# Experts with at most 96 tokens as three rounds of 32 tokens, each in four column tiles of TensorE

## The chip, the cores and the metric

The kernel runs on one core of a Trainium2 chip. The metric is the device time of one execution in microseconds (us), from the first to the last instruction and what lies around it; lower is better.

## The reference, cut to what matters

One decoder layer on 1024 tokens of width 1024, all in float32: a mixer (projections, short convolution, sliding-window attention, output projection) and then a mixture of 32 experts, of which each token takes four. The experts are what the change touches:

```python
logits = h @ w_router + b_router                  # (1024, 32)
top_vals, top_idx = lax.top_k(logits, 4)
gates = softmax(top_vals)
# for every expert e, on the tokens routed to it:
hid = xb @ w1[e] + b1[e]                          # (n, 1024) @ (1024, 2048)
x_glu, x_lin = hid[..., ::2], hid[..., 1::2]
x_glu = min(x_glu, 7); x_lin = clip(x_lin, -7, 7)
act = x_glu * sigmoid(1.702 * x_glu) * (x_lin + 1)
yb = (act @ w2[e] + b2[e]) * gate                 # (n, 1024) @ (1024, 1024)
out[token] += yb
```

Evaluated on its own inputs, the reference routes 4096 token-expert pairs. The 32 experts get, sorted: 66, 80, 81, 93, 95, 95, 100, 101, 106, 113, 114, 122, 122, 123, 125, 126, 128, 134, 136, 136, 136, 137, 138, 140, 148, 152, 161, 163, 165, 172, 187, 201 tokens. So 15 have more than 128, 11 have 97 to 128, and 6 have at most 96.

## The kernel before, in words

`mixer` runs first, in eight blocks of 128 tokens. Two of its places serve later as comparisons. `route_quarters` (line 889) makes the router's logits with 32 stationary columns in each of four column tiles of TensorE, every tile with its own moving data of 128 columns. `attend` (L921) does the same with 64 stationary columns in two column tiles and 512 moving columns.

`experts` then runs one job for each expert (at most 256 tokens a job). Jobs are sorted on the chip by a key (L1463 to L1487), large ones first: `size` counts the limits 128, 136, ..., 208 that an expert's tokens exceed, the key is `past - 128 * size`, and `reached` compares the keys with `marks`, so that every engine reads from `ends` and `jobs` how many jobs there are of each kind. Jobs with over 128 tokens are wide: weights stationary, tokens moving (`piece`, L1686). Jobs with at most 128 are narrow, and run last: tokens stationary, 128 columns, weights moving. The work of one narrow job:

- SP (SyncE) loads w1 in four pieces of 2 MB (each 512 of the 2048 columns, all 1024 rows, in runs of 2 KB) and w2 in two such pieces into the six slots of `w_slot` (`load_pieces`, L1235). The load for a slot is issued when TensorE has used it (`w_used`), so weights arrive one job ahead. b1 and b2 are spread over 128 partitions (L1256, L1259).
- TensorE, `first_layer` (L1710): for each of the four chunks c, eight matmuls (k = 0..7) of 128x128 stationary x, 512 moving columns. Every float32 matmul stands in the trace as two MATMUL records, called passes below. `list_rows` (L1699) makes the token list of the next job between chunks 1 and 2. `second_layer` (L1722): eight matmuls of 512 columns for each half of the output. The last two k of both halves wait for the last chunk, turned by TensorE (`turn_last`, L1732).
- VectorE, for each chunk: add b1 (L1589), clip (L1593, L1594), multiply with ScalarE's sigmoid (L1601, L1604), and, but for the last, turn the rows into `act_T` by 32x32 transposes (L1216). After chunk 1 it takes over the next list (L1626 to L1582), which lets POOL (GpSimd) gather the next job's rows (L1293). At the end it turns the gathered rows into `xT` (L1216, `turn_x`), adds the gated b2 (L1636), and marks the tokens of the job after next (L1567 to L1572).
- ScalarE: sigmoids (L1394), the copy of the last chunk (L1397), b2 times gate (L1400).
- POOL adds the result to the output by an indirect DMA (L1337).

```python
def narrow_job(t, q):                 # TensorE, L1735
    first_layer(t, q, 0)
    first_layer(t, q, 1)
    list_rows(q + 1)
    first_layer(t, q, 2)
    first_layer(t, q, 3)
    second_layer(t, q, 0, range(0, KD - 2))
    turn_last(t)
    second_layer(t, q, 1, range(0, KD - 2))
```

## Time and profile before

| what | value |
|---|---|
| median of 3 runs | 2027.83 us (2026.98 to 2029.89) |
| the profiled execution, its own time | 2026.62 us |
| its span, first to last instruction | 2024.8 us |
| mean granted TensorE clock | 0.989 of 2.4 GHz |
| TensorE busy | 1970.9 us (97%) |
| from the first narrow job's start to the 17th's (1297.25 to 1966.87 us) | 669.6 us |

In a windows row stand the length, the busy us of PE, PEld, DVE, ACT and POOL with their counts, the granted clock, the DMA share and GB/s. A row of "busy" for TensorE counts modelled, overlapping ends: one pass of 512 columns is drawn as 592 ns, but the next one starts 429 ns after it. So durations below are taken between starts. In a timeline row the first number is the start, the second the length of the merged stretch, and "x32" the number of records in it; PE is the matmul side of TensorE and PEld its weight loads. DMA share is the mean busy share of the 16 DMA engines; overlapping packets can take it over 1.

### The profile page before, as it was taken

How to read it: one execution, taken by the hardware profiler on the slowest of the kernel's cores; microseconds unless marked ns; L12 is line 12 of the kernel's file. 1: busy time of each engine (PE TensorE's matmuls, PEld its weight loads, DVE VectorE, ACT ScalarE, POOL GpSimd, SP SyncE). 2: the span in 40 equal slices, each digit the busy share in tenths (PEclk: the TensorE clock that was granted, in tenths of full speed). 3: DMA queues.
4: the chain of work that ended last, by engine and by line, in shares of the span. 5: the costliest groups of instructions: out<-in, count | busy, mean ns of one | idle time of the engine just before them, and what ended most of it. 6: DMA issues, size and time to landing. Idle time of an engine off the chain costs nothing.

```text
span 2024.8 us, 29838 instructions
## 1 busy us (share of the span) xinstructions
PE 1970.9 (97%) x10536; PEld 1434.4 (71%) x10536; DVE 1424.0 (70%) x4050; ACT 402.7 (20%) x848; POOL 237.0 (12%) x317
## 2 busy tenths in 40 slices
PE   7999999997999999999999999999999999999996
PEld 5677777774999999999999999744444444444442
DVE  2777777764467777778766776777667776777765
ACT  1233333232012112222222223211100010000100
POOL 1221222221010011111111111100000000000000
PEclk8999999998999999999999999999999999999998
DMA  9311110004866778787788888999999999999992
GB/s 308 105 42 41 41 33 20 31 32 177 305 219 210 263 249 269 246 273 266 258 293 281 299 290 306 327 329 370 361 354 372 367 368 362 356 368 370 370 355 74
DMA packets 232238, 504.17 MB, mean 249 GB/s; under 512 B 7428, under 2 KB 14640, under 8 KB 230016
## 3 DMA queue, kind: packets, MB, share of 16 engines
q1 hardware_dynamic: 218496, 454.93, 62.9%
q0 software_dynamic: 11392, 40.18, 8.1%
q10 hardware_dynamic: 2304, 8.39, 1.0%
q8 instruction: 35, 0.57, 0.1%
q14 instruction: 11, 0.09, 0.0%
HBM read 475.48 MB, written 28.00 MB: 249 GB/s over the span
## 4 chain that ended last, share of the span: by engine, by line
issue 41%; PE 11%; DMA 1%; POOL 1%; DVE 1%; POOLq 0%; ACT 0%
PE ps_unit L1686 11%; DMA out_dram<-y_rows,idx_cur 1%; POOL x_got L1293 1%; DVE act_T L1515 0%; DVE sig L1513 0%; DVE glu L1505 0%; ACT sig L1376 0%; POOL carrier L1289 0%; POOL out_dram L1337 0%; POOL out_dram L1305 0%; PE ps_list L1658 0%; POOLq L1065 0%; POOLq L1227 0%; POOLq L1328 0%; DMA x_got<-h_rows,idx_next 0%
## 5 line engine op out<-in xcount | busy, mean ns | idle before, releaser
L1686 PE MATMUL ps_unit<-xT,w_slot 128*128 128x136 f32 (+6 forms) x3840 | 523.1, 299 | 1.6 <-DVE xT L1540 1.6
L1686 PEld LDWEIGHTS ps_unit<-xT,w_slot 128*128 128x128 f32 x3840 | 518.2, 197 | 2.0 <-issue 1.8
L1710 PE MATMUL ps_unit<-w_slot,xT 128*128 128x512 f32 x1088 | 473.9, 593 | 0.0
L1710 PEld LDWEIGHTS ps_unit<-w_slot,xT 128*128 128x128 f32 x1088 | 205.3, 190 | 251.6 <-issue 251.6
L1216 DVE STREAM_TRANSPOSE xT<-x_got 32x256 f32<-32x256 f32 x668 | 291.0, 436 | 15.9 <-DMA x_got<-h_rows,idx_next 7.1
L1686 PE MATMUL ps_unit<-act_T,w_slot 128*128 128x136 f32 (+6 forms) x1920 | 264.1, 299 | 10.4 <-DVE act_T L1515 10.3
L1686 PEld LDWEIGHTS ps_unit<-act_T,w_slot 128*128 128x128 f32 x1920 | 259.3, 191 | 13.9 <-DVE act_T L1515 7.3
L1722 PE MATMUL ps_unit<-w_slot,act_T 128*128 128x512 f32 x544 | 239.3, 592 | 1.3 <-DVE act_T L1216 1.3
L1216 DVE STREAM_TRANSPOSE act_T<-act_rows 32x64 f32<-32x64 f32 x816 | 192.6, 236 | 12.2
L1531 DVE STREAM_TRANSPOSE y_rows<-yT 32x256 f32<-32x256 f32 x396 | 172.6, 436 | 39.6 <-ACT yT L1383 34.4
L1722 PEld LDWEIGHTS ps_unit<-w_slot,act_T 128*128 128x128 f32 x544 | 102.0, 190 | 123.6 <-issue 121.5
L899 PE MATMUL ps_c<-hT,w_in_sb 128*128 128x128 f32 x1536 | 182.1, 279 | 4.5 <-DMA w_in_sb<-in_w_in_dram 4.5
L899 PEld LDWEIGHTS ps_c<-hT,w_in_sb 128*128 128x128 f32 x1536 | 177.4, 194 | 9.7 <-DMA w_in_sb<-in_w_in_dram 5.3
L1289 POOL TENSOR_TENSOR carrier<-carrier 128x1 f32<-128x1 f32 x64 | 14.9, 233 | 1362.0 <-issue 572.7
L1394 ACT ACTIVATE sig<-glu 128x256 f32<-128x256 f32 x68 | 28.3, 416 | 553.6 <-DVE glu L1593 553.6
L1589 DVE TENSOR_TENSOR hid<-ps_unit,b_row 128x512 f32<-128x512 f32 x68 | 47.0, 691 | 84.5 <-PE ps_unit L1710 84.4
L1513 DVE TENSOR_TENSOR sig<-sig,glu 128x256 f32<-128x256 f32 x120 | 50.9, 424 | 69.6 <-ACT sig L1376 61.3
L1376 ACT ACTIVATE sig<-glu 128x256 f32<-128x256 f32 x120 | 50.0, 417 | 243.6 <-DVE glu L1505 243.4
L1505 DVE TENSOR_SCALAR glu<-ps_unit,b_cur 128x256 f32<-128x256 f32 x120 | 57.5, 479 | 52.5 <-PE ps_unit L1686 52.0
L1383 ACT ACTIVATE yT<-ps_unit,b_cur 128x256 f32<-128x256 f32 x120 | 50.3, 469 | 210.2 <-PE ps_unit L1686 210.2
L1388 ACT ACTIVATE y_rows<-y_rows,gate_cur 128x1024 f32<-128x1024 f32 x30 | 32.8, 1141 | 179.5 <-DVE y_rows L1531 179.5
L1636 DVE SCALAR_TENSOR_TENSOR y_rows<-ps_unit,gate_cur,b_row 128x512 f32<-128x512 f32 x34 | 25.5, 751 | 59.8 <-PE ps_unit L1722 59.8
(267 smaller groups left out, 1648.4 us busy)
## 6 DMA issues: line engine op xcount, KB each, us to landing
w_slot<-in_w_dram SPq DMA_DIRECT2D x192, 2048.0 KB, 10.9
b_row<-in_b_dram SPq DMA_DIRECT2D x17, 1024.0 KB, 12.8
b_row<-in_b_dram SPq DMA_DIRECT2D x17, 512.0 KB, 15.1
w_in_sb<-in_w_in_dram SPq DMA_DIRECT2D x6, 1024.0 KB, 12.0
x_in<-in_x_dram SPq DMA_DIRECT2D x8, 512.0 KB, 3.5
x_res<-in_x_dram SPq DMA_DIRECT2D x8, 512.0 KB, 4.8
out_dram<-x ACTq DMA_DIRECT2D x8, 512.0 KB, 5.1
h_rows<-h ACTq DMA_DIRECT2D x8, 512.0 KB, 3.2
```

The lines of the kernel that those rows point to most:

```text
L899: last = pe.matmul(ps_c[:, c % 2, j * P:(j + 1) * P], w_in_sb[:, k, first:first + P], hT[:, k, :], start=(k == 0), stop=(k == KD - 1))
L1216: last = nc.vector.transpose(out[c * Q:(c + 1) * Q, :, tokens], rows.rearrange("p (k c j) -> p k c j", c=P // Q, j=Q)[:, :, c, :])
L1376: nc.scalar.activation(sig[:, p % 3, :], glu[:, p % 3, :], ACT.Sigmoid, scale=ALPHA).then_inc(sig_ready[p].sem, 1)
L1383: last = nc.scalar.activation(yT[:, m, :], ps_unit[p % RING][:, u, :], ACT.Identity, bias=b2_cur[:, m:m + 1])
L1388: last = nc.scalar.activation(y_rows[:, h, :], y_rows[:, h, :], ACT.Copy, scale=gate_cur[:, h:h + 1])
L1505: v.tensor_scalar(glu[:, p % 3, :], ps_unit[p % RING][:, 0, :], b1_cur[:, 2 * p:2 * p + 1], LIMIT, ALU.add, ALU.min).then_inc(glu_ready[p] ...
L1513: v.tensor_tensor(sig[:, p % 3, :], sig[:, p % 3, :], glu[:, p % 3, :], ALU.mult).then_inc(scaled[p].sem, 1)
L1531: last = v.transpose(rows[:, :, c, :], yT[c * Q:(c + 1) * Q, :, a * Q:(a + 1) * Q])
L1589: v.tensor_tensor(hid[:, c % 2, :], ps_hid[c], b1_row[:, c * LW:(c + 1) * LW], ALU.add).then_inc(hid_read[c].sem, 1)
L1686: last = pe.matmul(ps_unit[p % RING][:, u, 0:n], w, moving[:, k, 0:n], start=(k == 0), stop=(k == KD - 1))
L1710: last = pe.matmul(ps_hid[c], xT[:, k, 0:P], w_slot[:, c, k, :], start=(k == 0), stop=(k == KD - 1))
L1722: last = pe.matmul(ps_out[m], act_T[:, k, 0:P], w_slot[:, W1_LOADS + m, k, :], start=(k == 0), stop=(k == KD - 1))
```

## The change

Jobs with at most 96 tokens ("slim") get a kind of their own, between wide and narrow. A slim job's 96 token columns are three rounds t of 32 tokens. In a round, the 32 columns of x stand in four column tiles of the array at once (`tile_position=(0, g * 32)`), and tile g gets as moving data the g-th quarter of the weight's columns: 512 of w1, 256 of w2. The result of a round stands in one PSUM bank, partitions 32g to 32g+31 for tile g. The first layer's k loop is outermost up to k = 5, so that weights come as whole rows (runs of 8 KB for w1, 4 KB for w2). b1 is spread as four quarters over 32 partitions each, b2 over 96. The rows of a round are turned by TensorE and copied by ScalarE, VectorE's `act_T` transposes are gone; ScalarE moves the second layer's result, quarter by quarter, into `y_rows`. The sorting gets one more mark, and every engine one more job count.

```diff
+TILE = 32
+TILES = 3
+SLIM = TILES * TILE
...
+                        src = w1[0, bass.ds(e, 1), 2 * i * P:2 * (i + 1) * P, :].rearrange("o (k p) f -> p (o k) f", p=P)
+                        sp.dma_start(w_slot[:, i, :, :].rearrange("p (k c) f -> p k (c f)", k=2), src).then_inc(w_loaded[i].sem, 16)
...
+                    nc.gpsimd.indirect_dma_start(
+                        out=out_rows, out_offset=bass.IndirectOffsetOnAxis(ap=idx_cur[0:SLIM, 0:1], axis=0),
+                        in_=y_rows[0:SLIM, 0, :], in_offset=None, compute_op=ALU.add).then_inc(rows_moved.sem, 16)
...
+            def slim_read_act(s, t):
+                wait_round(act, slim_turned, s, t)
+                nc.scalar.copy(act_T[:].rearrange("p (g r) n -> p r g n", r=2)[:, :, :, t * TILE:(t + 1) * TILE],
+                               ps_act[:, 0:2, :].rearrange("p r (g n) -> p r g n", g=W1_LOADS)).then_inc(slim_actT.sem, 1)
...
+                for g in range(W1_LOADS):
+                    last = nc.scalar.copy(y_rows[t * TILE:(t + 1) * TILE, 0, g * PW:(g + 1) * PW],
+                                          ps_flat[TILES + t][g * TILE:(g + 1) * TILE, 0:PW])
...
+                    slim_sigmoid(s, 0)
+                    slim_sigmoid(s, 1)
+                    slim_read_act(s, 0)
+                    slim_sigmoid(s, 2)
+                    slim_read_act(s, 1)
...
+            then_wait(v.scalar_tensor_tensor(out=slim[:], in0=first[:], scalar=float(SLIM), in1=held[:], op0=ALU.add,
+                                             op1=ALU.is_ge))
+            then_wait(v.scalar_tensor_tensor(out=past[:], in0=slim[:], scalar=-float(P // 2), in1=past[:], op0=ALU.mult,
+                                             op1=ALU.add))
...
+                    wait(dve, gate_summed, q)
+                    wait(dve, pool_moved, wide - 1)
+                    wait(dve, rows_moved, s - 1)
+                    v.tensor_copy(idx_cur[:, 0:1], idx_next[:, 0:1])
...
+                    read_narrow_list(q + 1)
+                    for t in range(TILES):
+                        slim_clip_round(s, q, t)
+                        slim_finish_round(s, t)
+                    wait(dve, gathered_a, q + 1)
+                    turn_x(q + 1, P // Q)
+                    match_narrow(q + 2, bass.ds(e_next, 1), base_row[:, bass.ds(q + 2, 1)])
+                    wait(dve, slim_b2, s)
+                    wait_round(dve, slim_out_read, s, TILES - 1)
+                    v.scalar_tensor_tensor(out=y_rows[0:SLIM, 0, :], in0=y_rows[0:SLIM, 0, :], scalar=gate_cur[0:SLIM, 0:1],
...
+            def slim_first(t, k):
+                i, f = k // 2, k % 2
+                for g in range(W1_LOADS):
+                    w = w_slot[:, i, :, :].rearrange("p (k c) f -> p k (c f)", k=2)[:, f, g * LW:(g + 1) * LW]
+                    last = pe.matmul(ps_flat[t][g * TILE:(g + 1) * TILE, :], xT[:, k, t * TILE:(t + 1) * TILE], w,
+                                     start=(k == 0), stop=(k == KD - 1), tile_position=(0, g * TILE))
...
+                for k in range(KD - 2):
+                    if k % 2 == 0:
+                        wait(pe, w_loaded[k // 2], q)
+                    for t in range(TILES):
...
+                        last = slim_first(t, k)
...
+                    if k == 3:
+                        list_rows(q + 1)
+                wait(pe, w_loaded[W1_LOADS - 1], q)
+                for t in range(TILES):
+                    for k in (KD - 2, KD - 1):
+                        last = slim_first(t, k)
+                    last.then_inc(round_done.sem if t < TILES - 1 else w_used[W1_LOADS - 1].sem, 1)
+                slim_turn(s, 0)
+                slim_second(s, q, 0, range(0, 4))
+                slim_turn(s, 1)
+                slim_second(s, q, 0, range(4, KD))
+                slim_second(s, q, 1, range(0, 4))
+                slim_turn(s, 2)
+                slim_second(s, q, 1, range(4, KD))
+                slim_second(s, q, 2, range(0, KD))
```

`slim_turn` transposes a round's `act_rows` in two transposes of 128x128 into `ps_act`; `slim_second` is the second layer of a round, four matmuls of 256 columns for each k, one in each column tile; `slim_clip_round` and `slim_finish_round` are `clip_rows` and `finish_rows` for a round.

## Rows read from the trace of the kernel before

**Rows 1.** Page, part 1 and part 2: engines' shares; the span in 40 slices.
```profile
PE 1970.9 (97%) x10536; PEld 1434.4 (71%) x10536; DVE 1424.0 (70%) x4050; ACT 402.7 (20%) x848; POOL 237.0 (12%) x317
...
PEclk8999999998999999999999999999999999999998
DMA  9311110004866778787788888999999999999992
```
**Rows 2.** Windows: first narrow job, fifteen narrow jobs, 10 us (us, busy by engine, clock, DMA).
```profile
1297.25:1341.22 43.97, 42.19 (x108) 18.45 (x107) 36.33 (x110) 8.67 (x12) 4.34 (x5) 1.00 0.87 302
1341.22:1966.87 625.65, 625.65 (x1591) 279.16 (x1590) 451.19 (x1515) 65.53 (x105) 45.28 (x60) 1.00 1.02 365
1620.00:1630.00 10.00, 10.00 (x26) 4.54 (x25) 8.36 (x21) 3.12 (x4) 0.00 (x0) 1.00 1.06 392
```
**Rows 3.** Timeline of PE, one narrow job (columns: start, length, as above).
```profile
1508.06 13.90 PE L1710 MATMUL ps_unit<-w_slot,xT 128*128 128x512 f32 x32
1521.79 0.35 PE L1699 MATMUL ps_list<-entry,match 128*128 128x5 bf16 x8
1522.00 13.98 PE L1710 MATMUL ps_unit<-w_slot,xT 128*128 128x512 f32 x32
...
1540.97 0.38 PE L1732 MATMUL ps_act<-cst,act_rows 128*128 128x128 f32 x2
1541.18 8.75 PE L1722 MATMUL ps_unit<-w_slot,act_T 128*128 128x512 f32 x20
```
**Rows 4.** Timeline of PE in the mixer: two and four column tiles, and neighbours.
```profile
416.52 1.95 PE L899 MATMUL ps_c<-hT,w_in_sb 128*128 128x128 f32 x16
418.39 0.65 PE L889 MATMUL ps_s<-h2T,w_router_sb 128*32 128x128 f32 x16
418.97 0.71 PE L899 MATMUL ps_c<-hT,w_in_sb 128*128 128x128 f32 x4
...
444.09 1.94 PE L921 MATMUL ps_c<-pT,v_keys 128*64 128x512 f32 x8 [0.45 <-DVE pT L716]
445.95 1.55 PE L993 MATMUL ps_s<-w_out_sb,conv_s 128*128 128x512 f32 x3
```
**Rows 5.** Timeline of DVE and ACT in that narrow job.
```profile
1521.99 0.69 DVE L1589 TENSOR_TENSOR hid<-ps_unit,b_row 128x512 f32<-128x512 f32 x1 [0.33 <-PE ps_unit L1710]
...
1529.15 0.69 DVE L1589 TENSOR_TENSOR hid<-ps_unit,b_row 128x512 f32<-128x512 f32 x1
1529.88 0.29 DVE L1593 TENSOR_SCALAR glu<-hid 128x256 f32<-128x256 f32 x1
...
1531.64 3.98 DVE L1216 STREAM_TRANSPOSE act_T<-act_rows 32x64 f32<-32x64 f32 x16
...
1537.07 0.42 ACT L1394 ACTIVATE sig<-glu 128x256 f32<-128x256 f32 x1 [6.45 <-DVE glu L1593]
...
1538.39 7.17 DVE L1216 STREAM_TRANSPOSE xT<-x_got 32x256 f32<-32x256 f32 x16
...
1548.34 0.75 DVE L1636 SCALAR_TENSOR_TENSOR y_rows<-ps_unit,gate_cur,b_row 128x512 f32<-128x512 f32 x1 [2.77 <-PE ps_unit L1722]
...
1541.38 0.37 ACT L1397 COPY act_T<-ps_act 128x256 f32<-128x256 f32 x1 [3.90 <-PE ps_act L1732]
```
**Rows 6.** Timeline of POOL: the last scatter of the last wide job.
```profile
1312.30 1.33 POOL L1305 DMA_INDIRECT out_dram<-y_rows,idx_cur  x1 [0.30 <-issue]
```
**Rows 7.** DMA view from 1341 to 1967 us: KB each, median us to landing.
```profile
w_slot<-in_w_dram SPq DMA_DIRECT2D x90, 2048.0 KB, 13.1
out_dram<-y_rows,idx_cur POOLq DMA_INDIRECT x15, 9.9
x_got<-h_rows,idx_next POOLq DMA_INDIRECT x15, 7.0
```
**Rows 8.** Timeline of DVE in the sorting of the jobs.
```profile
476.47 0.16 DVE L1467 TENSOR_TENSOR past<-past,cst 128x1 f32<-128x1 f32 x1
476.66 0.16 DVE L1468 SCALAR_TENSOR_TENSOR order_key<-size,past 128x1 f32<-128x1 f32 x1
```

More of the change, by code:

```diff
@@ L1116, in experts @@
         order = sb("order", [P, P], BF16)
-        ends = sb("ends", [1, len(SIZES) + WORDS], I32)
-        ended, started, first, held, size, past = (sb(n, [P, 1]) for n in ("ended", "started", "first", "held", "size", "past"))
+        ends = sb("ends", [1, COLUMNS + WORDS], I32)
+        ended, started, first, held, size, past, slim = (
+            sb(n, [P, 1]) for n in ("ended", "started", "first", "held", "size", "past", "slim"))
         ps_unit = [ps(f"ps_unit{i}", [P, 2, CAP]) for i in range(RING)]
@@ L1207, in job_counts, with wait_round @@
             wide = eng.value_load(ends[0:1, last_size - 1:last_size], min_val=0, max_val=most_jobs)
+            slim_jobs = eng.value_load(jobs[0:1, 2:3], min_val=0, max_val=most_jobs)
             narrow_jobs = eng.value_load(jobs[0:1, 1:2], min_val=0, max_val=most_jobs)
-            return wide, narrow_jobs
+            full = eng.value_load(ends[0:1, len(SIZES):COLUMNS], min_val=0, max_val=most_jobs)
+            return wide, slim_jobs, narrow_jobs, full
+        def wait_round(eng, e, jobs_done, t):
+            eng.wait_ge(e.sem, e.of(jobs_done * e.per, t))
         def turn_squares(out, rows, tokens):
@@ L1238, in _ @@
             sp.wait_ge(rows_moved.sem, 16)
-            wide, narrow_jobs = job_counts(sp)
+            wide, slim_jobs, narrow_jobs, full = job_counts(sp)
             with sp.If(wide > 0):
@@ L1315, in _ @@
             get(gathered_b, 1, P)
-            wide, narrow_jobs = job_counts(pool)
+            wide, slim_jobs, narrow_jobs, full = job_counts(pool)
             with pool.If(wide > 0):
@@ L1648, in _ @@
             with dve.If(narrow_jobs > 0):
                 with dve.Fori(0, narrow_jobs) as t:
[L1650 removed]
+                    narrow_job(t, t + full)
         @block.tensor
@@ new lines, in slim_second @@
+            def slim_second(s, q, t, ks):
+                if ks[0] == 0:
+                    wait(pe, unit_read[RING + TILES + t], wide - 1)
+                    wait_round(pe, slim_out_read, s - 1, t)
+                    wait_round(pe, slim_actT, s, t)
+                for k in ks:
+                    i, f = W1_LOADS + k // 4, k % 4
+                    if t == 0 and f == 0:
+                        wait(pe, w_loaded[i], q)
+                    for g in range(W1_LOADS):
+                        w = w_slot[:, i, :, :].rearrange("p (k c) f -> p k (c f)", k=4)[:, f, g * PW:(g + 1) * PW]
+                        last = pe.matmul(ps_flat[TILES + t][g * TILE:(g + 1) * TILE, 0:PW], act_T[:, k, t * TILE:(t + 1) * TILE], w,
+                                         start=(k == 0), stop=(k == KD - 1), tile_position=(0, g * TILE))
+                    if t == TILES - 1 and f == 3:
+                        last.then_inc(w_used[i].sem, 1)
+                if t < TILES - 1 and ks[-1] == KD - 1:
+                    last.then_inc(slim_out.sem, 1)
@@ L1834, in _ @@
+            with pe.If(slim_jobs > 0):
                 with pe.If(wide < 1):
                     first_rows()
+                with pe.Fori(0, slim_jobs) as s:
+                    slim_job(s, s + wide)
+            full = wide + slim_jobs
+            with pe.If(narrow_jobs > 0):
+                with pe.If(full < 1):
+                    first_rows()
                 with pe.Fori(0, narrow_jobs) as t:
-                    narrow_job(t, t + wide)
+                    narrow_job(t, t + full)
```

203 lines of the change are left out of this document (171 added, 32 removed).

## The prediction

> **What bounds the kernel now.** First the page's parts 1 and 2: TensorE is busy in 97% of the span, at full clock over the part that matters (the last third of the slices), and the DMA engines stand at nine tenths or more there too [rows 1]. So one asks which of the two ends last. The windows of the narrow stage answer: in fifteen whole narrow jobs, 625.65 us, TensorE has no idle time, 625.65 / 15 = 41.71 us a job, while the DMA moves 365 GB/s at a share of 1.02, and in its best 10 us 392 GB/s [rows 2]. The timeline shows that TensorE's time is the passes alone: 32 passes of 512 columns from 1508.06 to 1521.79, that is 0.429 us each, 96 of them in a job (41.2 us), 0.21 us for the list and 0.21 us for the turn [rows 3]. A pass costs its moving columns, whether 66 or 128 of the 128 stationary columns hold tokens. TensorE is the bound, the DMA queue is close behind. VectorE's 451 us in those 625.65 are covered [rows 2].
>
> The reference's own routing gives 6 experts with at most 96 tokens, 11 with 97 to 128. So 6 of the 17 narrow jobs become slim; they come first, the first of them right behind the last wide job. The other 26 jobs keep their code.
>
> **TensorE's share of a slim job.** Removed: 96 passes. Added: in the first layer 3 rounds times 8 k, each k-step four matmuls of 512 columns, one in each column tile. If four tiles really run at once, a k-step costs two passes, 0.859 us: 24 x 0.859 = 20.6 us instead of 27.5. The second layer has 24 k-steps of 256 columns, 0.429 us each: 10.3 us instead of 13.7. In sum 30.9 us instead of 41.2.
>
> Do they run at once? Two rows show tiles with separate moving data. With four tiles and 128 columns, 16 passes take 418.97 - 418.39 = 0.58 us, where the 16 full-array passes of the same width ahead of them take 416.52 to 418.39, 0.117 us each; four at a time would be 0.47, so 0.11 us is over. With two tiles and 512 columns, 8 passes take 1.86 us, and two at a time would be 1.72: 0.14 over [rows 4]. The excess is nearly the same for a block of 0.5 and of 1.8 us, so I read it as a price of entering and leaving tiled work, 0.14 us a block, and the sharing itself as full. That is the value I take; from below nothing under 0.859 us is possible for 512 columns in one tile, from above no sharing would be four times that.
>
> The Trainium skill speaks against this: "TensorE: Matmul & The Clock Gate", section "Part 3: Packing small matmuls — row/col tiling", has three column tiles of 512 columns at 2.38 times and four row tiles at 3.07 times one, that is 0.77 to 0.79 of full. By it a k-step would cost 1.3 times what I take and a slim job would be no shorter than a narrow one; the traced blocks show no such loss, but both are short. It is the first rival below.
>
> Full-array work inside the tiled work: the list (0.21 us) and three turns of two transposes (0.21 us each), each with 0.14 us for the change-over, 0.35 us a block [rows 3, 4]. With the list the first layer ends at 20.6 + 0.35 = 20.95 us after the job's start. Then one wait is open. Round 0 is complete four k-steps earlier, at 17.5; VectorE picks a finished bank up 0.20 us after the next passes begin, and needs 1531.64 - 1529.15 = 2.49 us a round [rows 3, 5]: rounds end at 20.2, 22.7 and 25.2. TensorE turns round 0 by 21.3, but ScalarE's copy into `act_T` is queued behind the sigmoid of round 1, for which VectorE must first add and clip (0.69 + 0.29 from 20.2): sigmoid 0.42 to 21.7, copy 0.37 to 22.1 [rows 5]. So the second layer begins 1.2 us after the first, the turn of round 0 included. The turns of rounds 1 and 2 come when their rows have long been ready (24.2 against 22.7, 28 against 25.2) and cost 0.35 us each. Sum: 20.95 + 1.2 + 10.3 + 0.7 = 33.2 us.
>
> **What must stay covered.** VectorE loses the three `act_T` transposes (3.98 us each) [rows 5]. Its chain to the next `xT` is 25.2 + 7.17 = 32.4 us, against TensorE's 33.2: covered by 0.8 us. That needs the next rows to be there by 25.2. The chain for them: behind the last pass ScalarE copies four quarters (4 x 0.37), VectorE adds b2 over 1024 columns (about 2 x 0.75 us) [rows 5], POOL issues the addition, which lands 9.9 us later [rows 7], about 13.6 us into the next job. Only then may VectorE overwrite `idx_cur`, which now stands ahead of its first round, take the list, and let POOL gather: 7.0 us [rows 7], landed at about 21.3, 3.9 us in time. `idx_cur` itself is free at 13.6, round 0 wants VectorE at 17.7. ScalarE's twelve copies of 0.37 us and its sigmoids are under 10 us a job. All this is covered, but by few us where now it is tens.
>
> **The DMA.** A narrow job moves 6 x 2048 KB of weights, 1536 KB of biases, 1024 KB of rows: 15.2 MB, which is 365 GB/s over 41.71 us, so the view is accounted for [rows 2, 7]. A slim job moves 12288 + 256 + 384 + 512 + 384 KB = 14.2 MB: 38.8 us at 365 GB/s, 36.1 us at 392. Both exceed 33.2, so the queue falls behind by 3 to 6 us with each slim job. It has a cushion: loads are issued a job ahead, the last slots are freed at the end of a job and wanted 22 us into the next, which with the job's own length leaves some 24 us, against 13.1 us to landing now [rows 7]: 11 us to spare, more for the first slots. Over the five loads behind slim jobs 12 to 25 us may gather, so a stall of 0 to 14 us at their end is possible. Longer runs (8 and 4 KB for 2 KB) may shift the rate either way; no row shows by how much. I take 0.6 us a job, 3 us in all, for this and late gathers: 33.8 us a slim job. SP's extra issues (four for b1) stand behind the load of slot 3 and ahead of slots that are freed 10 us later; the wait for the b2 row (3.2 us into a job) comes ahead of slot 0's release at 5.2.
>
> **The first slim job** meets the scatter of the last wide job: it must have landed (1312.30 + 9.9 = 1322.2, 24.9 us into the job [rows 6, 7]) ahead of VectorE's round 0, where before it stood after chunk 1. Round 0 then ends at 28.0, the copy at 29.9, the job at 29.9 + 10.3 + 0.7 = 40.9 us; before, that first job took 43.97 [rows 2]. Saved: 3.1. The sorting adds two dependent VectorE steps at a cadence of 0.19 us [rows 8], two more small ones and one register load per engine: between 0 (hidden behind the gather of the first rows) and 2 us; I take 1.0.
>
> **Sum.** 5 x (41.71 - 33.8) + 3.1 - 1.0 = 41.6 us. The profiled execution took 2026.6 us, 1.2 us under the median: 1985.0 on its basis, 1986.2 on that of the median, and 1986 is what I forecast.
>
> **Rivals.**
> 1. *The tiles share worse in long runs.* Place: the 48 k-steps. A job is then 30.9 f + 2.3 us, and it decides at f = (41.7 - 2.3) / 30.9 = 1.27. At f = 1.3 a job is 42.5 us and the first, whose VectorE wait is then covered, also 42.5: 5 x 0.8 - 1.5 + 1.0 = 3.5 us slower, 2031 us; with tiles two at a time (f = 2) 64.1 us a job, 2160 us. For it: no row has four tiles with 512 columns, each moving stream being read at once. Against: the four-tile block and the two-tile block show an excess that doesn't grow with length [rows 4]. 0.09.
> 2. *The supply ends last*: the DMA keeps 365 GB/s and its cushion is gone at once, or the scatter-gather chain with 3.9 us to spare is late. A slim job is then 38.8 us: 5 x 2.9 + 3.1 - 1.0 = 16.6 us saved, 2011 us; half of it 1998. For it: a share of 1.02 already now [rows 2]. Against: the cushion, and fewer bytes. 0.14.
> 3. *Short instructions bind.* The second layer wants a weight load and a pass every 54 ns. The row of the list has 8 such pairs in 0.21 us, 26 ns each, straight behind long passes [rows 3]: nothing against it, but they came from a filled queue. The Trainium skill, "TensorE: Matmul & The Clock Gate", section "Wait — 56ns, not 53.3ns?", gives 62 ns a matmul where the sequencer decodes in software; by it the second layer would be 11.9 us and the forecast 8 us higher, 1994 us. At half of the list's pace, 52 ns, it costs nothing. It lies inside the forecast's own range and has no separate time there; 0.05 of its chance.
> 4. *The change doesn't take hold*: the sort on the chip counts none as slim. 2029 us, 0.03. The counts nearest to 96 are 95 and 100, far for rounding.
>
> **The numbers.** Forecast 0.74, rival 2 0.14, rival 1 0.09, rival 4 0.03. The forecast's own range is 1974 (no allowance, waits half of what I charge, the first job without its wait) to 1998; to hold 8 in 10 the range takes in rival 2: 1974 to 2011. About 0.2% (4 us) is what a measurement can tell from no change. Faster 0.74 + 0.14 = 0.88, same 0.03, slower 0.09.
>
> **What the profile after would show.** Right: six stretches of about 33 to 35 us, 192 passes of 512 columns and 192 of 256 in each, the start of a k-step 0.86 and 0.43 us after the last one's; about 1.2 us of TensorE's idle time behind the first layer; the first slim job near 41 us. Wrong: k-steps above 1.09 us (rival 1); TensorE waiting for `w_slot` or `xT` (rival 2); k-steps of the second layer alone above 0.43 us (rival 3); 17 jobs with 128 stationary columns (rival 4).

## The result and the profile after

The changed kernel takes 2001.68 us (median of 4 runs, 1999.35 to 2003.95), the kernel before 2028.06 us beside it (4 runs): ratio 0.9871, 95% interval 0.9859 to 0.9883. It is faster by 26 us, 1.3%, where 42 were forecast. In the two profiled executions the spans are 1997.6 and 2024.8 us, 27.2 us apart.

First the page of the kernel after, parts 1 and 2. It looks like that of before [rows 1]: TensorE at 96%, the DMA at nine tenths in the last third. What is new stands in slices 28 to 32: 379 to 399 GB/s, where before there were 354 to 372.

```profile
span 1997.6 us, 33413 instructions
...
PE 1923.2 (96%) x12288; PEld 1402.9 (70%) x12288; DVE 1342.6 (67%) x3731; ACT 430.5 (22%) x926; POOL 236.0 (12%) x317
...
PEclk9999999999999999999999999999999999999998
DMA  9311101013867777777788888889999999999992
GB/s 309 109 42 42 42 12 41 31 32 119 327 204 243 255 244 268 255 264 259 265 278 287 287 305 290 311 300 381 399 388 379 382 364 358 365 368 368 366 356 74
```

The last line of the kernel before:

```profile
GB/s 308 105 42 41 41 33 20 31 32 177 305 219 210 263 249 269 246 273 266 258 293 281 299 290 306 327 329 370 361 354 372 367 368 362 356 368 370 370 355 74
```

The windows of the six slim jobs and the two narrow jobs behind them (cut where TensorE begins a job's first layer; the columns are us, then busy us and instructions by engine, granted clock, DMA share, GB/s) answer to [rows 2]:

```profile
1298.62:1341.10 42.48, 35.03 (x399) 13.67 (x402) 22.77 (x60) 10.42 (x20) 4.34 (x5) 0.92 0.80 292
1341.10:1374.67 33.57, 32.97 (x402) 13.13 (x398) 17.33 (x54) 8.95 (x20) 2.88 (x4) 1.00 1.00 381
...
1441.84:1475.41 33.57, 32.97 (x402) 13.12 (x398) 16.38 (x48) 9.06 (x20) 2.85 (x4) 1.00 1.02 394
1475.41:1510.92 35.51, 33.16 (x402) 13.00 (x394) 16.62 (x49) 9.06 (x20) 2.86 (x4) 1.00 1.03 381
1510.92:1564.32 53.40, 47.11 (x110) 20.28 (x107) 28.91 (x91) 7.10 (x12) 2.85 (x4) 0.90 1.04 385
1564.32:1606.03 41.71, 41.71 (x107) 18.61 (x106) 30.08 (x101) 4.37 (x7) 3.02 (x4) 1.00 1.03 374
```

So the first slim job takes 42.48 us, the next four 33.58 each, the sixth 35.51. And the first *narrow* job behind them takes 53.40 us, though its code is that of the others, which take 41.71 as before. The account in spans: the small jobs start 1.4 us later than before (1298.62 against 1297.25); the first six of them take 212.3 us instead of 252.5, so 40.2 saved; the seventh costs 11.7 more. 40.2 - 11.7 - 1.4 = 27.1 us.

Where the idle time in this is, TensorE's waits say (from 1298 us on: what it executed, on what it waited, us in all, times, longest):

```profile
PE ps_act L2052 <- DVE act_rows L1802: 6.5, 1, 6.5
PE ps_unit L1907 <- DVE act_T L1262: 6.3, 2, 3.8
PE ps_unit L2040 <- issue: 4.0, 6, 1.0
PE ps_unit L2040 <- DMA w_slot<-in_w_dram: 1.8, 1, 1.8
```

TensorE's timeline of the first slim job's end, the second one up to its second layer, and the first narrow job (start, us, and in brackets the idle time ahead and what ended it) stands beside [rows 3]:

```profile
1326.32 0.69 PE L2052 MATMUL ps_act<-cst,act_rows 128*128 128x128 f32 x2 [6.46 <-DVE act_rows L1802]
1328.00 3.64 PE L2040 MATMUL ps_unit<-w_slot,act_T 128*32 128x256 f32 x32 [0.99 <-issue]
...
1341.10 10.48 PE L2024 MATMUL ps_unit<-w_slot,xT 128*32 128x512 f32 x96
1351.52 0.35 PE L1877 MATMUL ps_list<-entry,match 128*128 128x5 bf16 x8
1351.80 10.51 PE L2024 MATMUL ps_unit<-w_slot,xT 128*32 128x512 f32 x96
1362.24 0.44 PE L2052 MATMUL ps_act<-cst,act_rows 128*128 128x128 f32 x2
1363.28 1.93 PE L2040 MATMUL ps_unit<-w_slot,act_T 128*32 128x256 f32 x32 [0.60 <-issue]
...
1510.92 14.00 PE L1894 MATMUL ps_unit<-w_slot,xT 128*128 128x512 f32 x32
...
1538.78 1.88 PE L1907 MATMUL ps_unit<-w_slot,act_T 128*128 128x512 f32 x4
1543.17 3.68 PE L1907 MATMUL ps_unit<-w_slot,act_T 128*128 128x512 f32 x4 [2.51 <-DVE act_T L1262]
1550.63 3.78 PE L1907 MATMUL ps_unit<-w_slot,act_T 128*128 128x512 f32 x4 [3.78 <-DVE act_T L1262]
1554.20 0.63 PE L1917 MATMUL ps_act<-cst,act_rows 128*128 128x128 f32 x2
1554.63 9.86 PE L1907 MATMUL ps_unit<-w_slot,act_T 128*128 128x512 f32 x20
```

Two things are to be seen. The slim job's four tiles share fully: a k-step of the first layer is eight of these passes (two for each of its four matmuls), and 96 passes in 10.44 us make 0.870 us a k-step, where two full-array passes take 0.859. And idle time is paid twice: behind it the same four passes take 3.68 us instead of 1.88, at the lower level of the clock. The granted clock of these stretches is 0.50 behind the first slim job's gap and 0.52 behind the narrow job's:

```profile
1328.00:1331.50 3.50, 3.50 (x32) 1.54 (x32) 2.54 (x7) 0.42 (x1) 0.00 (x0) 0.50 1.00 410
1543.17:1546.70 3.53, 3.53 (x4) 1.17 (x4) 2.64 (x11) 0.42 (x1) 1.19 (x2) 0.52 1.05 387
```

In the first narrow job TensorE idles 6.29 us and is busy for 47.11 instead of 41.71: 6.3 + 5.4 = 11.7 us.

TensorE names VectorE as the one it waited for; VectorE's own timeline passes it on, to the 1 MB of the narrow job's b1 row, issued at 1510.5 and landed at 1530.1, 16 us after VectorE was free for it and 12.3 us after TensorE had the first chunk ready (1517.8):

```profile
1530.14 0.69 DVE L1716 TENSOR_TENSOR hid<-ps_unit,b_row 128x512 f32<-128x512 f32 x1 [16.28 <-DMA b_row<-in_b_dram]
```

### The profile page after: what moved, and what is told of

Read it like the earlier page. It is cut to its first block, busy times and chain, and to the rows that moved or that the text cites. A ratio compares the mean times of both kernels' runs of the same rounds, so it can differ in the third digit from the quotient of the medians.

```text
span 1997.6 us, 33413 instructions
## 1 busy us (share of the span) xinstructions
PE 1923.2 (96%) x12288; PEld 1402.9 (70%) x12288; DVE 1342.6 (67%) x3731; ACT 430.5 (22%) x926; POOL 236.0 (12%) x317
## 4 chain that ended last, share of the span: by engine, by line
issue 38%; PE 13%; POOL 1%; DMA 1%; DVE 1%; POOLq 0%; ACT 0%
PE ps_unit L1864 13%; DMA out_dram<-y_rows,idx_cur 1%; POOL x_got L1361 1%; DVE act_T L1642 0%; DVE sig L1640 0%; DVE glu L1632 0%; ACT sig L1457 0%; POOL carrier L1357 0%; PE ps_list L1836 0%; POOL out_dram L1418 0%; POOL out_dram L1373 0%; POOLq L1081 0%; POOLq L1273 0%; DMA x_got<-h_rows,idx_next 0%; POOLq L1409 0%
## 5 line engine op out<-in xcount | busy, mean ns | idle before, releaser
L1894 PE MATMUL ps_unit<-w_slot,xT 128*128 128x512 f32 x704 | 306.7, 594 | 0.0
L1894 PEld LDWEIGHTS ps_unit<-w_slot,xT 128*128 128x128 f32 x704 | 132.8, 190 | 163.0 <-issue 163.0
L1907 PE MATMUL ps_unit<-w_slot,act_T 128*128 128x512 f32 x352 | 159.8, 607 | 6.3 <-DVE act_T L1262 6.3
L1262 DVE STREAM_TRANSPOSE act_T<-act_rows 32x64 f32<-32x64 f32 x528 | 124.6, 236 | 7.9
L1907 PEld LDWEIGHTS ps_unit<-w_slot,act_T 128*128 128x128 f32 x352 | 67.4, 195 | 88.3 <-issue 79.7
L2024 PE MATMUL ps_unit<-w_slot,xT 128*32 128x512 f32 x1152 | 126.0, 593 | 0.0
L1457 ACT ACTIVATE sig<-glu 128x256 f32<-128x256 f32 x120 | 50.0, 417 | 242.3 <-DVE glu L1632 242.1
L1475 ACT ACTIVATE sig<-glu 128x256 f32<-128x256 f32 x44 | 18.3, 416 | 371.9 <-DVE glu L1720 371.9
L2024 PEld LDWEIGHTS ps_unit<-w_slot,xT 128*32 128x32 f32 x1152 | 36.7, 110 | 80.1 <-issue 79.2
L1716 DVE TENSOR_TENSOR hid<-ps_unit,b_row 128x512 f32<-128x512 f32 x44 | 30.4, 692 | 68.0 <-PE ps_unit L1894 51.7
## 6 DMA issues: line engine op xcount, KB each, us to landing
w_slot<-in_w_dram SPq DMA_DIRECT2D x192, 2048.0 KB, 11.7
```

The costliest lines, as they stand in the source:

```text
L1262: last = nc.vector.transpose(out[c * Q:(c + 1) * Q, :, tokens], rows.rearrange("p (k c j) -> p k c j", c=P // Q, j=Q)[:, :, c, :])
L1457: nc.scalar.activation(sig[:, p % 3, :], glu[:, p % 3, :], ACT.Sigmoid, scale=ALPHA).then_inc(sig_ready[p].sem, 1)
L1716: v.tensor_tensor(hid[:, c % 2, :], ps_hid[c], b1_row[:, c * LW:(c + 1) * LW], ALU.add).then_inc(hid_read[c].sem, 1)
L1894: last = pe.matmul(ps_hid[c], xT[:, k, 0:P], w_slot[:, c, k, :], start=(k == 0), stop=(k == KD - 1))
L1907: last = pe.matmul(ps_out[m], act_T[:, k, 0:P], w_slot[:, W1_LOADS + m, k, :], start=(k == 0), stop=(k == KD - 1))
L2024: last = pe.matmul(ps_flat[t][g * TILE:(g + 1) * TILE, :], xT[:, k, t * TILE:(t + 1) * TILE], w, start=(k == 0), stop=(k == KD - 1), tile_ ...
```

## The experiments

Two theories stood at the start. **A, the queue:** slim jobs ask for bytes faster than the DMA brings them; the loads fall behind job by job, and what has least time between issue and use shows it first, at the end of the slim jobs. **B, the hand-over:** the change from slim to narrow costs by itself, whatever ran before. Ratios are to the kernel before on the same chip. Its own median was 2028.5 us beside the first four kernels, 2029.6 beside the next three, 2027.3 beside the last four, so medians of different groups can't be compared to better than some 2 us; the spans from the start of the small jobs to the end of the profiled executions are the finer measure. In the changed kernel that is 1997.6 - 1298.6 = 699.0 us.

**Three slim jobs instead of six.**

```diff
-            then_wait(v.scalar_tensor_tensor(out=slim[:], in0=first[:], scalar=float(SLIM), in1=held[:], op0=ALU.add,
+            then_wait(v.scalar_tensor_tensor(out=slim[:], in0=first[:], scalar=82.0, in1=held[:], op0=ALU.add,
```

> Only experts with at most 82 tokens are slim: three slim jobs and fourteen narrow ones instead of six and eleven; nothing else changes. Theory A (queue): every slim job leaves the loads some 2.7 us further behind, so after three of them the first narrow job finds its b1 row in time. First slim job 42.5 us, the next two 33.58 us, no wait for a weight slot, first narrow job 41.7 to 43 us instead of 53.4. Time: 2001.7 + 3 x (41.71 - 33.58) - 11.7 - 1.75 = about 2012.6 us, so three slim jobs fewer cost only 11 us. Theory B (hand-over): the change from slim to narrow costs some 11 us however many slim jobs ran before. First narrow job about 53 us again, time 2001.7 + 24.4 - 1.75 = about 2024 us.

Measured: 2012.15 us, ratio 0.9925 (0.9908 to 0.9941). The first narrow job takes 43.45 us, with one wait of 0.53 us and one of 0.51:

```profile
1434.84 3.60 PE L1907 MATMUL ps_unit<-w_slot,act_T 128*128 128x512 f32 x8
1438.97 1.98 PE L1907 MATMUL ps_unit<-w_slot,act_T 128*128 128x512 f32 x4 [0.53 <-DVE act_T L1262]
```

B falls: the same change of kind, and no 11 us. The run also prices the later slim jobs: the last three save (2012.15 - 2001.68) / 3 = 3.5 us each instead of 8.1.

**The first narrow job's b1 row ahead of its weights.** The slim jobs get a b1 buffer of their own.

```diff
...
+                e = expert_of(sp, full)
+                spread_b1(e)
+                narrow_loads(0, full, e, True)
...
-                last = v.tensor_tensor(hid[:, t % 2, :], ps_flat[t], b1_row[:, 0:LW], ALU.add)
+                last = v.tensor_tensor(hid[:, t % 2, :], ps_flat[t], b1_slim[:], ALU.add)
```

> Six slim jobs as in the changed kernel. The slim jobs' b1 rows get a buffer of their own, so that the b1 row of the first narrow job waits for no slim job and is issued ahead of that job's weight loads instead of behind three of them. Theory A: the row lands before VectorE wants it, the first narrow job takes 42 to 44 us instead of 53.4; 1 MB more stands ahead of the weights in the queue, so their loads may be late by 0 to 3 us. Time 1990 to 1993 us. Theory B (the change of kind costs by itself): first narrow job 53 us whatever the row does, time about 2002 us. A third: the queue as a whole is behind, and the late row only shows it first; then the weights' loads end the first narrow job's waits instead, and it takes 46 to 50 us, time 1995 to 1999 us.

Measured: 1998.62 us, ratio 0.9858 (0.9842 to 0.9875), not to be told from the changed kernel's; from the start of the small jobs it is 695.0 us, 4 less. The first narrow job now takes 41.81 us, and the second 50.30: the wait has moved by one job, to the next b1 row in the old place. VectorE's timeline:

```profile
1571.84 0.69 DVE L1726 TENSOR_TENSOR hid<-ps_unit,b_row 128x512 f32<-128x512 f32 x1 [14.77 <-DMA b_row<-in_b_dram]
```

So neither A's 1990 nor B's 2002 us; the third case, that the whole queue is behind, is nearest, though it was again the row and not the weights that came late.

**VectorE takes the token list over behind round 0.**

```diff
-                    v.tensor_copy(idx_cur[:, 0:1], idx_next[:, 0:1])
...
-                    read_narrow_list(q + 1)
                     for t in range(TILES):
                         slim_clip_round(s, q, t)
                         slim_finish_round(s, t)
+                        if t == 0:
...
+                            v.tensor_copy(idx_cur[:, 0:1], idx_next[:, 0:1])
...
+                            read_narrow_list(q + 1)
```

> Only VectorE's order in a slim job changes: the copies of the next job's token list and gates, which wait for GpSimd's scatter of the job before, stand behind round 0's two additions instead of ahead of them. In the first slim job that wait let TensorE idle 6.46 us. If the wait for the last wide scatter is what that job pays for, its idle time falls to about 3 us (round 1 then waits for the same scatter) and it takes about 39 us instead of 42.5; the others stay at 33.58 us. Time: 1998.5 us if the rest of the chain follows, 2001 to 2002 us if the queue gives it back at the sixth job or the first narrow one (theory A: what TensorE gains earlier, the late loads take back at the end of the stage).

A miss: 2018.04 us, ratio 0.9957 (0.9941 to 0.9973), 16 us slower than the changed kernel. The ten executions spread from 2009.61 to 2025.45 us, and the profile is of the fastest, so it accounts for only 9.3 us (708.3 us from the start of the small jobs to the end); what the slower ones lose besides was not seen. VectorE of the second slim job, then TensorE at the start of the third:

```profile
1362.93 0.15 DVE L1816 COPY idx_cur<-idx_next 128x1 int32<-128x1 int32 x1
...
1372.61 7.18 DVE L1262 STREAM_TRANSPOSE xT<-x_got 32x256 f32<-32x256 f32 x16 [4.28 <-DMA x_got<-h_rows,idx_next]
```

```profile
1380.13 12.14 PE L2025 MATMUL ps_unit<-w_slot,xT 128*32 128x512 f32 x96 [3.08 <-DVE xT L1262]
```

The list that is read there is also what GpSimd gathers the next rows by. In the changed kernel VectorE reads it 13.3 us into a slim job (1354.42 in the job begun at 1341.10), here 20.5 us (1363.17 in that begun at 1342.68). That sends the gather off late in *every* slim job, and TensorE waits for `xT` at the start of each following job: 1.8 us in the second slim job and the first narrow one, 3.1 to 3.5 us in the four between. The slim jobs behind the first take 37.5 to 39.5 us. In the first one the idle time only fell to 5.5 us, and it took 43.2 us where 39 were expected. At that slower pace the first narrow job takes 41.81 us: no backlog. The steady slim job, which the expectation left at 33.58, was the step overlooked.

**Slim jobs last.** The order is wide, narrow, slim.

```diff
...
             then_wait(v.scalar_tensor_tensor(out=slim[:], in0=first[:], scalar=float(SLIM), in1=held[:], op0=ALU.add,
-                                             op1=ALU.is_ge))
+                                             op1=ALU.is_lt))
...
```

On every engine the block of the narrow jobs stands ahead of that of the slim ones, with the semaphore counts that go with it.

> The narrow jobs run right after the wide ones and the slim jobs last; the work of each kind is the same. Theory A: no narrow job follows a stretch of slim ones, so the 11.7 us of the late b1 row are gone; the first slim job follows a narrow one and takes about 34 us instead of 42.5; the first narrow job takes 44 instead of 41.7 us; a late weight load of 1 to 3 us in the fifth or sixth slim job stays. The kernel's tail may be 0 to 2 us longer. Time: 2001.7 - 11.7 - 8.9 + 2.3 + 1.5 = about 1985 us. Theory B: the change from narrow to slim costs as much as that from slim to narrow, time about 1995 to 1998 us.

Measured: 1999.54 us, ratio 0.9863 (0.9847 to 0.9879), where A's reckoning had about 1985. No loss at the change (the last narrow job 41.80 us, the first slim one 33.51), so B is out in this direction too; but A's size was wrong. The loads come late inside the slim jobs now, from the third on, 11.6 us of waits for a slot in all. The stretch from 1851 to 1966 us is three slim jobs long, cut at the same place of a job each time. Its window, and its DMA view (share and GB/s in 40 slices, then packets):

```profile
1851.47:1965.67 114.20, 102.92 (x1194) 40.65 (x1195) 49.11 (x142) 27.14 (x60) 8.57 (x12) 0.96 1.02 374
```

```profile
DMA  9999999999999999999999999999999999999999
GB/s 303 277 413 416 428 416 433 372 312 283 364 409 406 359 242 369 416 416 425 422 428 362 265 365 406 412 389 231 331 422 425 416 425 425 386 259 319 409 409 407
DMA packets 8183, 42.74 MB, mean 374 GB/s; under 512 B 629, under 2 KB 629, under 8 KB 5111
```

This is a number that was missing: 42.74 MB in 114.20 us are 14.25 MB and **38.07 us a slim job** when, in this kernel, the supply alone sets the pace. TensorE needs 33.58, so each job adds 4.5 us of backlog, not 2.7. In the changed kernel the queue was quicker at the same share. Its window over the second to the sixth slim job:

```profile
1341.10:1510.92 169.82, 165.06 (x1994) 65.52 (x1986) 83.09 (x243) 44.98 (x100) 14.30 (x20) 1.00 1.02 386
```

At 386 GB/s the 14.25 MB take 36.9 us, which makes 3.3 us of backlog a job. What makes the two rates differ was not tried, so a slim job adds somewhere from 3.3 to 4.5 us. With 4.5 the changed kernel's loss comes out: if about three jobs' worth is cushion, three more jobs' 13.5 us stand against the 1.9 and the 11.7 us that were lost. That the two agree so closely is partly luck. The rate is that of another kernel. The cushion is fitted to the runs (in this one the waits begin in the third slim job already), and 5.4 of the 11.7 us are TensorE's slower passes and not a wait for bytes. The runs with three and with six slim jobs put it a little lower: 1.9 us lost with three (the first narrow job 43.45 us, the third slim job 33.69), 13.6 with six, 3.9 us for each of the last three.

**Fewer bytes, the same work.** Left out: half of the second layer's weights in the slim jobs; the old contents of the slots stand in for them.

```diff
...
-                        src = w2[0, bass.ds(e, 1), 4 * i * P:4 * (i + 1) * P, :].rearrange("o (k p) f -> p (o k) f", p=P)
...
+                        src = w2[0, bass.ds(e, 1), 4 * i * P:(4 * i + 2) * P, :].rearrange("o (k p) f -> p (o k) f", p=P)
...
```

> Leaves out half of the second layer's weights in the slim jobs: each of their two second-layer loads brings two of its four k-blocks (1 MB instead of 2 MB), and the old contents stand in for the rest; TensorE, VectorE, ScalarE and GpSimd do exactly the same work. Supply theory, as the runs so far sharpen it: a slim job of 33.58 us asks for 14.2 MB, which take the saturated queue 38.07 us, so each slim job adds 4.5 us of backlog; three jobs' worth is cushion and the other three come out as 1.75 + 11.7 us of waits. With 12.2 MB a job the queue needs some 32.5 us and no backlog builds: no wait for a weight slot, first narrow job 41.7 us, time 2001.7 - 13.4 = 1988.3 us (1987 to 1990). Hand-over theory (the change of kind costs by itself): first narrow job still about 53 us, time 1999 to 2002 us.

Measured: 1989.04 us, ratio 0.9806 (0.9785 to 0.9826); 1988.3 was worked out. No wait for a slot, and a first narrow job of 41.81 us:

```profile
1510.45 14.00 PE L1894 MATMUL ps_unit<-w_slot,xT 128*128 128x512 f32 x32
...
1538.31 5.31 PE L1907 MATMUL ps_unit<-w_slot,act_T 128*128 128x512 f32 x12
...
1552.26 3.17 PE L1894 MATMUL ps_unit<-w_slot,xT 128*128 128x512 f32 x7
```

Nothing but bytes was changed, so it is the queue's load that costs the 13 us (12.6 by the spans: 686.4 us from the start of the small jobs, against 699.0).

Where it strikes, SyncE's timelines show, of the changed kernel and of this one:

```profile
1486.63 23.57 SPq L1281 DMA_DIRECT2D w_slot<-in_w_dram  x4
1510.48 5.05 SPq L1322 DMA_DIRECT2D b_row<-in_b_dram  x1
```

```profile
1482.28 16.25 SPq L1281 DMA_DIRECT2D w_slot<-in_w_dram  x4
1500.19 1.51 SPq L1322 DMA_DIRECT2D b_row<-in_b_dram  x1
```

With fewer bytes each of the four issues takes 0.37 us, the row is issued 10.3 us ahead of its job and lands 13.0 us later, some 4 us before it is wanted. In the changed kernel three of the four issues take 10.7, 6.8 and 5.2 us, the row is issued 0.4 us ahead of its job, though VectorE had read the row before it by 1498.7, and it lands 19.6 us later. So of the 16.4 us that the row loses, 9.8 are lost before SyncE has issued it and 6.6 in the queue.

**The b1 row in two halves, each issued as soon as its half is free.**

```diff
...
-                        if i == W1_LOADS - 1:
...
-                            sp.dma_start(b1_row[:], src.partition_broadcast(P)).then_inc(b1_loaded.sem, 16)
+                        if i in (1, W1_LOADS - 1):
+                            wait(sp, hid_read[i], t - 1 if i < W1_LOADS - 1 else t + slim_jobs - 1)
+                            part = slice((i - 1) * LW, (i + 1) * LW)
...
+                            sp.dma_start(b1_row[:, part], src.partition_broadcast(P)).then_inc(b1_loaded[i // 2].sem, 16)
...
```

The slim jobs' b1 rows have a buffer of their own here too.

> The same bytes, in another order: the narrow job's b1 row (1 MB, issued behind the fourth weight load and wanted some 21 us later) goes in two halves, each issued as soon as its half has been read by the job before, some 34 us ahead of its use; the slim jobs' b1 rows have a buffer of their own. Supply theory, with the b1 row as the transfer that has least time between issue and use: the backlog of six slim jobs is carried into the narrow stage and is worked off there, where a job needs 41.7 us on TensorE and less in the queue. First and second narrow job 41.7 to 44 us, the 1.75 us at the sixth slim job stays; time 2001.7 - 11.7 = 1990 us (1989 to 1993). If the weights' own loads are as late as the row, they wait in its place: narrow jobs of 44 to 50 us, time 1995 to 1999 us, as with the row of the first narrow job alone moved (1998.6 us).

Measured: 1995.81 us, ratio 0.9839 (0.982 to 0.9858), above the 1989 to 1993 expected. All narrow jobs take 41.71 to 41.81 us, so the backlog is carried over and costs nothing there. The sixth slim job takes 37.71 us instead of 35.51: a wait of 2.62 us and slower passes behind it. From the start of the small jobs to the end it is 689.9 us, against 699.0 in the changed kernel: 9.0 saved. The medians differ by only 5.9, since the small jobs here began 3.0 us later (1301.66 against 1298.62), see below.

**No slim job at all:** what is left of the change is its sorting and its code.

```diff
-            then_wait(v.scalar_tensor_tensor(out=slim[:], in0=first[:], scalar=float(SLIM), in1=held[:], op0=ALU.add,
+            then_wait(v.scalar_tensor_tensor(out=slim[:], in0=first[:], scalar=1.0, in1=held[:], op0=ALU.add,
```

> The threshold is set so low that no job is slim: all seventeen small jobs are narrow, and what remains of the change is the added sorting and set-up. Sorting alone costs what the start of the stage showed, 1.4 us: first narrow job 44.0 us, sixteen more at 41.71 us, time 2028.1 + 1.0 to 1.4 = 2029.3 us (2028.5 to 2030). If the added code also costs in the other stages, more than 2030 us.

Measured: 2034.07 us (7 runs), ratio 1.0032 (1.0017 to 1.0046), 3 to 9 us over before, where 1.0 to 1.4 were expected. The profile is of the fastest of the seven (2030.73 to 2038.71 us); its span is 4.1 us over, and this is the account: TensorE's last wide passes begin 2.3 us later than before (1286.28 against 1283.94); then TensorE idles 3.77 us where it passes over the slim block that it doesn't run; the first narrow job, whose waits are covered by that, takes 41.81 instead of 43.97. So the gap costs less than 2 us net.

```profile
1303.53 13.99 PE L1894 MATMUL ps_unit<-w_slot,xT 128*128 128x512 f32 x32 [3.77 <-issue]
```

No such gap stands between the kinds where both run. What the 3.77 us are was not tried.

**The slim jobs keep their token list in a buffer of their own,** on the kernel with the halves. Then VectorE needn't wait for the last wide scatter ahead of round 0; ScalarE waits for it ahead of its first output row.

```diff
...
+                    wait(act, pool_moved, wide - 1)
...
-                    wait(dve, pool_moved, wide - 1)
...
-                    v.tensor_copy(idx_cur[:, 0:1], idx_next[:, 0:1])
...
+                    v.tensor_copy(idx_slim[:], idx_next[:, 0:1])
...
```

> The kernel with the b1 row in halves, and the slim jobs keep their token list and gates in a buffer of their own, so that VectorE no longer waits in the first slim job for the last wide job's scatter (that scatter is awaited by ScalarE ahead of its first write of the output rows). TensorE's idle 6.5 to 6.8 us in the first slim job go away. If a microsecond gained on TensorE were a microsecond of time: 1995.8 - 6.6 = 1989.2 us. Supply theory: the queue is busy throughout the slim jobs and delivers their bytes no sooner, so what the first slim job gains comes back as waits for a weight slot in the fifth and sixth; time 1994 to 1996 us, the waits for a slot up from 2.6 us to some 9 us.

Measured: 1987.45 us, ratio 0.9808 (0.978 to 0.9837), 8.4 us under the halves alone (6 us by the two ratios, as it ran on another chip); from the start of the small jobs it is 685.7 us instead of 689.9, 4.2 us less. Its four executions spread from 1982.4 to 1992.0 us. The supply theory's forecast, that the queue would take the gain back, failed. The first slim job takes 37.09 us instead of 42.70, the second 35.10 instead of 33.60 (TensorE now waits 3.40 us for `xT`), and the sixth is as it was: 37.88 against 37.71. The windows of the first job, with the halves alone and with both edits, point to the reason:

```profile
1301.66:1344.36 42.70, 34.88 (x399) 13.60 (x399) 22.65 (x60) 10.42 (x20) 4.34 (x5) 0.92 0.79 290
```

```profile
1298.94:1336.03 37.09, 33.19 (x400) 13.04 (x399) 22.54 (x59) 13.20 (x25) 4.39 (x5) 1.00 0.98 353
```

The DMA share is 0.79 in the one, 0.98 in the other. I read it so: in the first slim job the queue is not behind yet; while TensorE idles, no slot comes free, and the queue has less to do. A stall there delays both, and taking it away wins for both.

**The same buffer, on the kernel with fewer bytes** (again without half of the slim jobs' second-layer weights).

> The same buffer of its own for the slim jobs' token list, put on the kernel whose slim jobs leave out half of the second layer's weight bytes (1989.0 us). There the queue is not behind, so by the supply theory the 6.8 us of idle time in the first slim job are a real gain: no wait for a slot, time 1989.0 - 6.8 = 1982.2 us (1981 to 1984). Without the supply theory this and the edit on the kernel with all its bytes gain the same.

Measured: 1981.40 us, ratio 0.9783 (0.976 to 0.9806). The time is the forecast one, but the gain isn't: from the start of the small jobs it is 681.2 us instead of 686.4, so 5.2 us gained where 6.8 were forecast (TensorE waits 2.80 us for `xT` at the second slim job), against 4.2 with all bytes. The two gains are nearly the same, which the expectation named as the mark against its own theory. By my reading of the two windows above it speaks against that theory only for the first slim job.

**Three slim jobs ahead of the narrow ones, three behind.**

```diff
...
+            slim_stage(late_jobs, narrow_jobs)
...
+            then_wait(v.scalar_tensor_tensor(out=slim[:], in0=first[:], scalar=82.0, in1=held[:], op0=ALU.add,
+                                             op1=ALU.is_ge))
...
```

> All bytes, all work, in another order: the three slim jobs of at most 82 tokens run ahead of the narrow jobs and the three others behind them (one more kind in the sort, 0.3 to 1 us). Supply theory: two stretches of three slim jobs with eleven narrow ones between, in which the queue catches up, lose nothing to the backlog but the 1.7 us that the first narrow job lost after three slim ones. From the start of the small jobs: 42.6 + 33.6 + 33.7 + 43.5 + 10 x 41.71 + 3 x 33.6 + 15.1 behind the last first layer's job = 686.3 us, against 698.9 us in the changed kernel: time 2001.7 - 12.6 + 0.7 = 1989.8 us (1988 to 1992). Hand-over theory (each change of kind costs some 11 us): two changes instead of one, time 2010 us or more.

Measured: 1992.40 us, ratio 0.983 (0.981 to 0.9849), just above the 1988 to 1992 expected. From the start of the small jobs it is 689.9 us instead of 686.3. The jobs are as expected (42.52, 33.57, 33.69, then 43.39); the error is the end: behind the start of its last job this kernel needs 52.5 us, where the sum had 33.6 + 15.1 = 48.7. Of the difference 1.3 us are a wait for a weight slot in that job; the rest is a longer tail behind TensorE's last pass. Two changes of kind, and still 9 us less than the changed kernel: B is out here too.

**Both, and the halves.**

> The split order with the b1 row in halves and the slim jobs' own token list. Three slim jobs leave cushion in the queue, so here the 6.5 us of the first slim job should largely be kept, and the first narrow job take 41.8 us. Time by the supply theory: 1989.8 - 6.5 - 1.7 = 1981.6 us; as the earlier start takes 6.5 us of the 13.4 us of cushion that three slim jobs use, 0 to 5 us of it may come back as waits: 1981 to 1987 us.

Measured: 1986.88 us, ratio 0.9804 (0.9782 to 0.9826), no different from the 1987.45 us without the split, and at the upper end of what was expected (1981 to 1987). The second slim job takes 36.35 us, again with a wait for `xT` (3.61 us), and the end is longer by those 3.7 us.

## Why the prediction was right and wrong

The time, 2001.7 us, lies outside the forecast's own range (1974 to 1998) and inside the stated one (1974 to 2011), which had been widened for rival 2. The gain was 26 us of the 42 forecast.

*Full sharing of the four tiles:* right. A k-step of the first layer is 0.870 us where 0.859 was taken, f = 1.013; the second layer's 24 k-steps take 1374.67 - 1363.28 = 11.39 us less two turns of 0.36, so (11.39 - 0.72) / 24 = 0.44 us each where 0.429 was taken. Rival 1 would have needed 1.27. By the Trainium skill ("TensorE: Matmul & The Clock Gate", "Part 3: Packing small matmuls — row/col tiling"), with 0.77 to 0.79 of full for three column tiles and for four row tiles, a k-step would be some 1.1 us, which is an estimate from the page's figures; the trace doesn't agree for four column tiles of 512 columns, where it is 0.870. Rival 3 is out too: a second-layer pass and its load come every 56 ns, 10.7 us in all.

*The slim job:* right. 21.14 us to the turn (20.95 predicted), 1.04 for turn and wait (1.2), then 11.39 (11.0): 33.58 us, between the 33.2 of the sum and the 33.8 charged.

*Vector work, gather and scatter:* covered, as said, by few us. VectorE takes the list over 13.1 us into the second slim job (13.6 predicted), and TensorE never waits for `xT`, so the part of the 3 us that was meant for late gathers was not needed. The run with the later takeover showed how few.

*The first slim job:* 42.48 us, 40.9 predicted. The wait is as long as worked out: the turn of round 0 begins 27.7 us into the job (28.0 predicted). What the step left out is the clock behind 6.5 us of idle time: 32 passes in 3.64 us instead of 1.93, TensorE busy 35.03 us instead of 32.97. That is 2.1 us.

*Sorting and set-up:* 1.0 taken, 1.4 seen, but the small jobs began anywhere from 1297.1 to 1303.9 us in the profiles of these kernels, so the term can't be read to a microsecond from one execution. No slim job at all costs 4.1 us in the profiled execution, 2.3 of it ahead of the passed-over block.

*The step that failed is the DMA's term in the sum:* "I take 0.6 us a job, 3 us in all, for this and late gathers." Its own bounds had the truth: "3 to 6 us with each slim job" (3.3 to 4.5, worked out from the two rates), "a stall of 0 to 14 us at their end" (13.6, most of it one job further on). Three things were mis-sized or missed in taking 3: the rate, the transfer that is short of time, and the clock. The rate: 36.1 to 38.8 us a job were the bounds, 36.9 is what it was in the changed kernel and 38.07 with the slim jobs last; neither leaves room for 0.6 us a job once the cushion is gone. The cushion was credited to the weight slots, and they did lose only 1.75 us; it was not asked which transfer has *least* time between issue and use, nor whether SyncE could issue it in time. That is the b1 row of the first job *behind* the slim ones: issued at 1510.5 behind four weight loads whose issues were themselves held up, wanted at 1517.8 when TensorE's first 16 passes of that job were through, landed at 1530.1. And each us of idle time there cost nearly two, by the clock. With what was measured in each place the sum reads 5 x (41.71 - 33.58) + 1.5 - 1.4 - 1.9 - 11.7 = 27.2 us: 5 steady jobs, the first job (43.97 - 42.48), the later start, the sixth job (35.51 - 33.58), the first narrow one.

*Rival 2* (the supply ends last, 2011 us, or half of it, 1998) names the mechanism that cost the 13 us; the result lies between it and the forecast. It was half right: the supply does not set the pace of all slim jobs; its backlog comes due only once the cushion is used up, behind the third job by the run with three slim jobs.

## What to carry to other kernels

When a change shortens the jobs of one kind below what the DMA can bring in that time, count the backlog to the end of the stretch, and look for the transfer with the least time between its issue and its use, in the *next* kind of job too: there the bill comes. A busy queue can also hold the engine that issues (0.37 us an issue in the run with fewer bytes, up to 10.7 us in the changed kernel): look at how long its issues take, and put the urgent transfer ahead of them. Issuing that transfer earlier, without moving a byte less, won 9 us here by the spans (6 by the medians). Taking a wait out of a stretch in which the queue isn't behind yet won 4 to 5 more (both together 1987 us against 2002); the DMA share of that stretch, 0.79 with the wait and 0.98 without it, is what told it from the later ones, at 1.00 to 1.03. An operation moved out of the way of one wait must be asked what else hangs on it: the token list read 7 us later cost 9 us in the profiled execution and 16 in the median.

## What was not expected of the hardware

The queue brought 374 GB/s over three slim jobs at a DMA share of 1.02, in slices of 2.9 us from 231 to 433: many stand over 410, but the troughs between them pull the mean down to near the narrow stage's 365 [rows 2]. In the changed kernel's slim jobs it brought 386 at the same share. What the troughs are was not tried. SyncE's own issue of a load, 0.37 us with fewer bytes, took 10.7 us at 1487 us, at a DMA share of 1.03 in that job, and what stood behind it on SyncE was late. Idle time cost TensorE more than itself: 6.5 us in the first slim job brought 2.1 us of slower passes, 6.3 us in the first narrow job 5.4. And a block of code that is passed over came with 3.77 us of idle time, where the same block run through showed none.
